# Second attention: the output banks are swapped, the first scores begin with the 512-key part, and one weight split moves from head 0 to the entry

## What is computed

```
kv = (c_kv @ w_ukv).reshape(B, L, MLA_HEADS, MLA_NOPE + MLA_V)      # 16 heads, 64 + 64
q = (c_q @ w_uq).reshape(B, L, MLA_HEADS, MLA_NOPE + MLA_ROPE)      # 64 + 32 rotary
s = (jnp.einsum('bqhd,bkhd->bhqk', qn, k_nope)
     + jnp.einsum('bqhr,bkr->bhqk', qr, k_rope)).astype(jnp.float32) * scale
p = jax.nn.softmax(jnp.where(mask, s, -jnp.inf), axis=-1)
return jnp.einsum('bhqk,bkhd->bqhd', p.astype(v.dtype), v)
```

## Time and profile before

| | |
|---|---|
| median of 3 runs | 2137.04 us (2136.07 to 2137.77) |
| profiled execution, its own time | 2137.52 us |
| its span in the trace | 2135.7 us |
| PE busy | 2079.1 us, 97% |
| PE weight loads busy | 1856.5 us, 87% |
| DVE, ACT, POOL busy | 1086.6, 775.8, 1104.8 us |
| second attention | from about 765 to 920 us of the span |

### The profile page before, as it was taken

The page is one execution under the profiler, slowest core; times in us unless marked ns, Lnnn a source line. Parts: engine busy times, 40 slices in busy tenths (PEclk is TensorE's granted clock), DMA queues, the critical chain, the costliest instruction groups (busy, mean ns, idle before and its releaser), DMA issues.

```text
span 2135.7 us, 38613 instructions
## 1 busy us (share of the span) xinstructions
PE 2079.1 (97%) x13834; PEld 1856.5 (87%) x13834; DVE 1086.6 (51%) x1881; ACT 775.8 (36%) x1287; POOL 1104.8 (52%) x1362
## 2 busy tenths in 40 slices
PE   7999899999999999999999999999999999999998
PEld 6888799999999977799999999777778778888886
DVE  6666754424236757754444236866512455335154
ACT  3433524323223367734313223434332224322233
POOL 5444345545556612145555556745455756546554
PEclk9999999999999999999999999999999999999999
DMA  5222122232323311122232322322233332323322
GB/s 180 66 73 78 60 80 87 82 99 80 98 87 93 104 33 41 31 75 85 93 94 86 100 88 98 99 79 79 69 99 97 110 99 89 109 89 92 98 85 79
DMA packets 51513, 184.87 MB, mean 87 GB/s; under 512 B 5712, under 2 KB 5840, under 8 KB 51408
## 3 DMA queue, kind: packets, MB, share of 16 engines
q1 hardware_dynamic: 50400, 181.49, 27.1%
q10 hardware_dynamic: 1008, 1.89, 0.3%
HBM read 181.26 MB, written 2.10 MB: 86 GB/s over the span
## 4 chain that ended last, share of the span: by engine, by line
PE 89%; DVE 7%; issue 2%; ACT 1%; DMA 0%; DVEq 0%; SPq 0%; ACTq 0%
PE ps L584 28%; PE ps L585 27%; PE ps L586 27%; PE ps L789 2%; DVE small L1214 1%; PE ps L701 1%; DVE scratch L1231 1%; PE ps L732 1%; PE ps L716 1%; PE ps L965 1%; DVE x_hi L1012 1%; DVE scratch L1199 0%; DVE scratch L1225 0%; PE ps L648 0%; DVE x_lo L1014 0%
## 5 line engine op out<-in xcount | busy, mean ns | idle before, releaser
L558 POOL TENSOR_TENSOR w_lo<-w_raw,w_hi 128x256 fp32r<-128x256 f32 x1352 | 1100.2, 847 | 1009.5 <-ACT w_hi L1594 1009.5
L584 PE MATMUL ps<-x_hi,w_hi 128*128 128x264 f32 (+2 forms) x2696 | 861.5, 320 | 8.9 <-issue 5.7
L585 PE MATMUL ps<-x_lo,w_hi 128*128 128x264 f32 (+2 forms) x2696 | 849.4, 315 | 0.0
L586 PE MATMUL ps<-x_hi,w_lo 128*128 128x264 f32 (+2 forms) x2696 | 848.3, 315 | 0.0
L584 PEld LDWEIGHTS ps<-x_hi,w_hi 128*128 128x128 f32 x2696 | 509.4, 189 | 57.1 <-issue 16.8
L585 PEld LDWEIGHTS ps<-x_lo,w_hi 128*128 128x128 f32 x2696 | 509.0, 189 | 34.1 <-issue 0.5
L586 PEld LDWEIGHTS ps<-x_hi,w_lo 128*128 128x128 f32 x2696 | 509.1, 189 | 32.0
L1594 ACT ACTIVATE w_hi<-w_raw 128x1024 fp32r<-128x1024 f32 x338 | 353.2, 1051 | 315.2 <-PE ps L586 308.7
L584 PE MATMUL ps<-g_hi,w_hi 128*128 128x264 f32 (+2 forms) x1312 | 408.0, 311 | 5.0 <-issue 4.1
L585 PE MATMUL ps<-g_lo,w_hi 128*128 128x264 f32 (+2 forms) x1312 | 405.8, 309 | 0.0
L586 PE MATMUL ps<-g_hi,w_lo 128*128 128x264 f32 (+2 forms) x1312 | 405.4, 309 | 0.0
(11 more groups left out here) (213 smaller groups left out, 1709.7 us busy)
## 6 DMA issues: line engine op xcount, KB each, us to landing
w_raw<-stream SPq DMA_DIRECT2D x338, 512.0 KB, 3.5
h<-x_t SPq DMA_DIRECT2D x4, 528.0 KB, 8.3
out_t<-h SPq DMA_DIRECT2D x8, 256.0 KB, 2.7
scratch<-rotary_tables ACTq DMA_DIRECT2D x4, 264.0 KB, 5.5
par<-params ACTq DMA_DIRECT2D x1, 342.0 KB, 4.9
scratch<-positions ACTq DMA_DIRECT2D x1, 256.0 KB, 2.7
cst<-shape_constants ACTq DMA_DIRECT2D x1, 193.0 KB, 6.5
```

The costliest lines, as they stand in the source:

```text
L558: last = nc.gpsimd.tensor_tensor(w_lo[:, j % 4, cols], w_raw[:, j % 4, cols], w_hi[:, j % 4, cols].bitcast(F32), ALU.subtract)
L584: nc.tensor.matmul(out_ap, w_hi[:, s, c], xh[:, k, cols], start=first, stop=False)
L585: nc.tensor.matmul(out_ap, w_hi[:, s, c], xl[:, k, cols], start=False, stop=False)
L586: return nc.tensor.matmul(out_ap, w_lo[:, s, c], xh[:, k, cols], start=False, stop=last)
```

## The change

Three edits. (1) The outputs of units 0 and 1 go to bank 3, those of units 2 to 4 to bank 2. (2) The scores of unit 0 begin with the 512-key part (bank 3) and then do the 16 meta keys (bank 2). The 512-key part waits only for outputs 0 and 1 of head h-2, the 16-key part for all five; unit 1 comes behind it and has no wait of its own. (3) ACT splits the half J_P+2 in the entry, before the first exponentials, instead of at the end of head 0; the placing of the rotary part of head 3 goes the other way.

```
-            bank = (2, 2, 3, 3, 3)[idx] if h + 1 < HEADS_B else (4, 4, 7, 7, 7)[idx]
+            bank = (3, 3, 2, 2, 2)[idx] if h + 1 < HEADS_B else (4, 4, 7, 7, 7)[idx]
...
                 wait(pe, exp_done_b, 5 * (h - 1) + group_end(idx))
-                if idx < 2:
-                    wait(pe, o_taken_b, 5 * (h - 1))
+                if idx == 0:
+                    wait(pe, o_taken_b, 5 * (h - 2) + 2)
                 s = scores_b(idx)
-                for k0, k1 in ((0, META), (META, META + P * t)) if idx == 0 else ((0, META + P * t),):
+                for k0, k1 in ((META, META + P * t), (0, META)) if idx == 0 else ((0, META + P * t),):
+                    if idx == 0 and k0 == 0:
+                        wait(pe, o_taken_b, 5 * (h - 1))
...
-                if h < 4:
+                if h == 0:
+                    place_rope(3)
+                elif h < 4:
                     hi_part(J_P + 2 + h)
...
-            place_rope(1), place_rope(2), place_rope(3)
+            place_rope(1), place_rope(2)
+            hi_part(J_P + 2)
             exps_b(0, 0), exps_b(0, 1)
```

## The result

The changed kernel takes 2125.38 us in the median of 5 runs (2125.03 to 2128.15); before, it was 2137.04 (2136.07 to 2137.77). The ratio is 0.9949, with a 95% interval of 0.9937 to 0.9962: faster by 8 to 13 us. The forecast was 2127.1, with 2125.8 to 2131.3. The ratio times the median before gives 2126.1, inside; the median of the runs itself lies 0.4 us under the low end. The profiled execution took 2126.15 us, its span is 2124.3 us.

A forecast was written before the change was run, and what follows sets the result against it. PE, busy 97% of the span, was taken to bound the kernel. -8.5 - 1.9 + 0.5 = -9.9 us from the profiled 2137.52 gives 2127.6; the runs' median lies 0.5 lower: 2127.1, range 2125.8 to 2131.3.

The forecast's parts named there:

- The first scores: Second attention, 14 places: PE no longer waits for DVE's output copies before unit 0's scores, 8.5 us saved.
- head 0 as control: Head 0 runs the same matmuls without the wait: last transpose to fill 1.53 us, against 2.17 with it.
- The rival of the idle column: First scores' waits: only the idle time shown comes back, 5.2 us instead of 8.5, giving 2130.6 us; chance 14%.
- Their place against S stays: DVE's output copies keep their time after S, the start of the last transpose, ending at S+0.53.
- the margin of 0.3 us: Before the 16-key part: copies let its load start at S+0.65, and it is due at S+0.97.
- the wait forms again: Rival before the 16-key part: copies slip 0.9 us, edits 1 and 2 bring nothing, 2135.6 us; chance 8%.
- The stop in head 1: PE's stop before a projection, waiting for POOL's work on J_P+2, goes: 1.9 us saved, bounds 1.7 and 2.2.
- The entry: Start of the second attention: POOL now runs beside DVE's scalings and delays PE, costing 0.5 us, bounds 0 and 0.9.
- the row of the cast: Nearest profile row for the entry's cost: a cast takes 0.85 us beside POOL and 0.42 without.
- DVE's spare time: Before the maxima: DVE gets scores 0.6 us earlier, and 0.4 us of its idle time is left in the shortest.

The follow-up runs named there:

- wait_back: The changed kernel, but the 512-key part waits for all five outputs again: median 2134.27 us, ratio 0.9990 to the kernel before.
- the changed kernel's first group: The changed kernel run once more, unaltered, beside the kernel before: median 2125.67 us, ratio 0.9948.
- late_copies: The changed kernel, but DVE scales units 2 to 4 before it copies outputs 2 to 4 of the older head: 2145.65 us, ratio 1.0048 to the kernel before.
- early_split: The changed kernel with the split of J_P+2 ahead of the two rotary parts in the entry: 2124.44 us, ratio 0.9944 to the kernel before.
- banks_mid: The kernel before plus edits 1 and 2, with J_P+2 split earlier in head 0, ahead of units 2 to 4's exponentials: 2126.66 us, ratio 0.9955.

## Why the prediction came out as it did

**The first scores: right, and the size too.** The step was 10 x 0.64 + 4 x 0.54 = 8.5 us. The changed kernel's traces have 1.53 us in all 15 heads. wait_back, which gives back only this wait, takes 132.83 - 124.97 = 7.9 us more for heads 0 to 14 and 0.5 more at the last place, 8.4 in all; its median is 8.6 us above the changed kernel's first group. Going by starts instead of the idle column (5.2 us) decided it, and head 0 as control was the row to trust. The rival of the idle column is refuted by the same runs.

**"Their place against S stays": true but for a few heads.** The copies end at S+0.52 to S+0.54 in ten places, at S+0.65 to S+0.71 in four, so the margin of 0.3 us is nearer 0.1 there. It held. late_copies shows what the rival "the wait forms again" would have cost: copies that end by S+0.81 cost nothing, and every tenth beyond that is paid in full, at each place.

**The stop in head 1: the step that was mis-sized.** I took 1.9 us, by 13.81 against 11.88, with 2.2 as the bound. In this one trace that is what it was. In four of six traces with such a stop the granted clock falls behind it and the head takes 15.3 us. Where it falls, the stop is worth 3.5 us: 136.3 - 132.82 for heads 0 to 14. The medians see mostly this case: edit 3 alone gave 2.9 us where 1.4 were expected. With 3.5 in place of 1.9 the sum is -8.5 - 3.5 + 0.5 = -11.5, against 11.7 and 11.1 measured. The range's low end was too high for the same reason: it took the first trace's clock for the kernel's. Nor did show a clock "granted in full in every slice", as I read it: the digit 9 says 90% or more, in slices of 53 us, and such a fall does not show in it. That trace itself has 0.83 in 40 to 60 us.

**Not additive, as said.** Of 136.3 us for heads 0 to 14 with the fall, edit 3 alone saves 3.5 us and edits 1 and 2 alone, also with the fall, 7.3; both together save 11.3. The missing 0.6 is the place in head 1, where without edit 3 an earlier PE only waits longer for the weights.

**The entry: 0.5 us, right, by a different division.** Going by the row of the cast, I made both scalings longer. In the trace the first takes it all (1.05 against 0.49) and the second nothing, and the first scaling ends at 769.73, 0.29 us behind POOL's last piece (769.44). early_split shows that the neighbour is the cause. The Trainium skill, SBUF — State Buffer, "Who interferes with whom", speaks of an exclusive lock, in which one operation stands until the other's instruction is through. The trace agrees: the delay, 0.56 us on the first scaling and 0.55 at PE, lies between the 0.5 of the cast's row and the 0.6 that I worked out by that rule.

**DVE's spare time: right.** The shortest idle time before the maxima is 0.38 us; 0.4 was forecast.

## What to carry to other kernels

When an engine's wait is priced, take the distance between starts, and compare it with a place in the same trace where the wait is absent. The idle column measured 0.40 us for what cost 0.64. And before a long stop of TensorE is priced from one trace, look at a second one: here, what came behind the stop ran at half the clock in four of six traces, and the first trace was one of the other two.

## What the runs showed of the hardware

After a stop of 2.2 to 2.8 us in TensorE, the granted clock fell to 1.2 GHz in four of six traces and cost 1.5 us; in the two traces shown step by step, the 4.3 us up to the stop's end held 2.0 and 2.3 us of matmul work. After the stop of 1.7 us in banks_mid it did not fall. That is no threshold: in late_copies, whose heads each have a stop of 0.5 to 1.8 us, it fell once, in head 3. The Trainium skill, TensorE: Matmul & The Clock Gate, "Part 1: The HAM clock gate", ties the clock to how busy the engine has been. The traces agree in so far as none without the long stop has a fall in head 1; that two executions of one program differ is shown here too.

A weight load that was released by a semaphore in the middle of a running group started 0.05 us behind its releaser's end (815.84 against 815.79); at the head of a group it was 0.12 (821.15 against 821.03).

A scaling of 128x528 beside POOL's pieces of 0.7 us took 1.05 us instead of 0.49.
